# Cross-attention output and feed-forward in one block: first products by pieces, the last two chunk pairs as one down product, the final norm on VectorE

## The reference, cut to what matters

```python
x = x + cross_attend(...)                 # ends in o @ w_xo
h = rmsnorm(x, g_ffn)
a, g = h @ w_up, h @ w_gate               # 1024 -> 2816 each
c = conv_b + sum(ext[:, i:i+t] * conv_w[i] for i in range(3))   # ext = [prev, a]
x = x + (gelu(c) * g) @ w_down            # 2816 -> 1024
y = rmsnorm(x, g_final)
```

## Time and profile before

| | |
|---|---|
| median of 3 runs | 2283.32 us (2280.44 to 2283.92) |
| profiled execution, its own time | 2284.99 us |
| its span | 2283.0 us |
| mean granted clock of TensorE, as a share of 2.4 GHz | 0.952 |
| cross output, first to last product | 1341.8 to 1458.4 us |
| first matmul of the feed-forward | 1489.65 us |
| first down matmul behind the last gate product | 2201.96 us |

### The profile page before, as it was taken

How to read it: one execution, slowest core, us unless ns; L and a number is a source line. 1 busy time by engine, 2 the same in 40 slices (tenths; PEclk the granted TensorE clock), 3 DMA queues, 4 the chain that set the end, 5 groups by cost and what they waited for, 6 DMA issues and landing times. The chain is left out here.

```text
span 2283.0 us, 27161 instructions
## 1 busy us (share of the span) xinstructions
PE 2086.4 (91%) x10848; PEld 1661.7 (73%) x10848; DVE 794.5 (35%) x1804; ACT 544.1 (24%) x1226; POOL 253.3 (11%) x110
## 2 busy tenths in 40 slices
PE   7989989569999997998998899589999999999995
PEld 4555548357677775665667546389999999999994
DVE  3001132345555454351003212333433443433446
ACT  2112220035455555000002101121122111122113
POOL 0000000000000000000000001132233222233322
PEclk9999999779899898999999999799999999999997
DMA  5521017530010003012102420011111101111102
GB/s 198 138 84 42 0 59 185 146 125 24 23 46 23 23 0 129 1 38 110 46 28 111 184 94 0 0 60 38 56 56 56 47 29 38 56 56 56 47 14 76
DMA packets 96244, 144.96 MB, mean 63 GB/s; under 512 B 40877, under 2 KB 72685, under 8 KB 94253
## 3 DMA queue, kind: packets, MB, share of 16 engines
q1 hardware_dynamic: 92062, 140.43, 18.3%
q10 hardware_dynamic: 4088, 3.17, 0.5%
HBM read 132.43 MB, written 14.26 MB: 64 GB/s over the span
## 5 line engine op out<-in xcount | busy, mean ns | idle before, releaser
L1678 PE MATMUL ps<-ff_in_high,ff_weights_high 128*128 128x352 f32 x1056 | 341.8, 324 | 18.7 <-POOL ff_weights_low L1637 18.7
L1678 PE MATMUL ps<-ff_in_low,ff_weights_high 128*128 128x352 f32 x1056 | 339.5, 322 | 0.0
L1678 PE MATMUL ps<-ff_in_high,ff_weights_low 128*128 128x352 f32 x1056 | 339.2, 321 | 0.0
L1678 PEld LDWEIGHTS ps<-ff_in_high,ff_weights_high 128*128 128x128 f32 x1056 | 199.0, 188 | 19.7 <-POOL ff_weights_low L1637 19.7
L1678 PEld LDWEIGHTS ps<-ff_in_low,ff_weights_high 128*128 128x128 f32 x1056 | 199.2, 189 | 0.0
L1678 PEld LDWEIGHTS ps<-ff_in_high,ff_weights_low 128*128 128x128 f32 x1056 | 198.8, 188 | 0.0
L1806 DVE TENSOR_TENSOR x<-ps,x 128x352 f32<-128x352 f32 x264 | 138.2, 525 | 154.8 <-PE ps L1695 154.7
L935 PE MATMUL ps<-top,big 128*128 128x128 f32 (+1 forms) x1184 | 167.2, 289 | 13.2 <-ACT big L1037 7.2
L935 PEld LDWEIGHTS ps<-top,big 128*128 128x128 f32 (+1 forms) x1184 | 145.9, 194 | 32.3 <-ACT big L1037 15.5
L371 PE MATMUL ps<-big 128*128 128x512 f32 (+3 forms) x432 | 160.0, 532 | 6.2 <-DVE top L404 6.2
L1695 PE MATMUL ps<-ff_act_high,ff_down_high 128*128 128x352 f32 x480 | 154.9, 323 | 0.1
(11 more groups left out here) (276 smaller groups left out, 2887.1 us busy)
## 6 DMA issues: line engine op xcount, KB each, us to landing
ff_weights<-in_w_up SPq DMA_DIRECT2D x22, 512.0 KB, 4.1
ff_weights<-in_w_gate SPq DMA_DIRECT2D x22, 512.0 KB, 4.5
ff_down<-in_w_down SPq DMA_DIRECT2D x22, 512.0 KB, 3.6
x<-in_xt SPq DMA_DIRECT2D x6, 1408.0 KB, 12.1
big<-bias_rows SPq DMA_DIRECT2D x8, 960.0 KB, 4.6
top<-in_mem_kt SPq DMA_DIRECT2D x7, 1024.0 KB, 12.2
big<-in_w_tm SPq DMA_DIRECT2D x8, 652.0 KB, 16.2
top<-in_mem_v SPq DMA_DIRECT2D x5, 1024.0 KB, 17.2
```

Of the source, the lines that this page charges most:

```text
L1678: last = nc.tensor.matmul(K.bank[3 * s + x][:, 0:b - a], w[:, s, ws], h[:, k, a:b], start=k + n == 0, stop=k == KD - 1 and n == 2)
```

## The change

The two blocks become one function, `cross_output_and_ffn`. On each engine the code of the feed-forward follows that of the cross output with no meeting between.

- Join. The cross products go to banks 6, 7, 1, 4, the sum to bank 5. Chunk 0 is not made by `up_and_gate(0)`: for each piece x, as soon as `low_made` says it is split, PE makes the up and the gate part of that piece; the spread of piece 3 stands behind the products of piece 1. The weights of chunk 0 are split behind piece 1 of the norm (ACT and POOL). DVE signals `scaled` after each half of the 8 tiles, not after all. SP issues the first loads of the feed-forward after the last cross product.
- End. `down(9)` and `down(10)` become `last_down`: one product of 12 matmuls over four chunks for each output tile, over the four pieces `ENDS` (352, 352, 224 and 128 columns), in four banks. For the first four tiles nine of the twelve matmuls are made before the last chunk is ready.
- Final norm. Squares on ACT, all else on DVE (`norm.scale`, the 8 tiles with gain and root at once); ACT's gain multiply and POOL's part are gone. One transfer for each piece of y.

```diff
+ENDS = [(0, FREE3), (FREE3, 2 * FREE3), (2 * FREE3, 928), (928, T)]
...
+            sp.wait_ge(xo_done, PRODUCTS)
             sp.dma_start(prev, I["conv_prev"]).then_inc(small, 16)
...
-            for p, (a, b) in enumerate(PIECES[:2]):
-                sp.wait_ge(y, 2 * p + 2)
+            for p, (a, b) in enumerate(ENDS):
+                sp.wait_ge(norm.scaled, p + 1)
                 sp.dma_start(O["y"][:, :, a:b], K.XT[:, :, a:b]).then_inc(K.out_sem, 16)
...
+            def last_down():
+                chunks = tuple(range(FC - 4, FC))
+                pe.wait_ge(act_low, FC - 1)
+                pe.wait_ge(d_low_made, FC - 1)
+                pe.wait_ge(up_taken, FC)
+                for o in range(EARLY):
+                    if o == 3:
+                        pe.wait_ge(act_made, FC)
+                    down_part(K.bank[o], ENDS[0], o, chunks[:3], True, False)
+                pe.wait_ge(act_low, FC)
+                pe.wait_ge(d_low_made, FC)
+                for p in range(len(ENDS)):
+                    for o in range(KD):
+                        n = p * KD + o
+                        if n >= 4:
+                            pe.wait_ge(down_taken, LAST + n - 3)
+                        late = n < EARLY
+                        down_part(K.bank[n % 4], ENDS[p], o, chunks[3:] if late else chunks, not late, True).then_inc(down_done, 1)
+                        if p and o == 3:
                             norm.spread(pe, p - 1)
...
+            for x in range(3):
+                pe.wait_ge(low_made, 2 * x + 2)
+                for s, done in enumerate((up_done, gate_done)):
+                    last = products(0, s, x)
+                    if x == 2:
+                        last.then_inc(done, 1)
+                if x == 0:
+                    pe.wait_ge(added, PRODUCTS)
+                    xnorm.spread(pe, 2)
             up_and_gate(1)
-            for g in range(PAIRS - 1):
+            for g in range(PAIRS - 2):
                 up_and_gate(2 * g + 2)
...
+            up_and_gate(FC - 2)
+            up_and_gate(FC - 1)
+            last_down()
...
+            dve.wait_ge(down_taken, LAST)
+            for p, (a, b) in enumerate(ENDS):
+                for o in range(KD):
+                    n = p * KD + o
+                    dve.wait_ge(down_done, LAST + n + 1)
+                    nc.vector.tensor_tensor(K.XT[:, o, a:b], K.bank[n % 4][:, 0:b - a], K.XT[:, o, a:b], ALU.add).then_inc(down_taken, 1)
+                    if p and o == 1:
+                        norm.add_up(dve, p - 1)
+                    if p and o == 5:
+                        norm.scale(dve, p - 1, lambda c, a, b: K.XT[:, c, a:b])
```

More of the change, by code:

```diff
@@ L1262, in _ @@
                     last.then_inc(xq_done, 1)
[L1266 to L1330, removed]
@@ L1591, in ffn @@
     down_done, down_taken = S("ff_down_product"), S("ff_down_taken")
[L1592 to L1595, removed]
+    norm = FeatureNorm(nc, K, "fin", K.XT, K.gains[:, 5, :], ENDS, [sq], root, K.bank[5])
+    PRODUCTS = 3 * KD
     TILE = 3 * KD
-    LAST = (PAIRS - 1) * TILE
-    TAIL = 6
+    LAST = (PAIRS - 2) * TILE
+    EARLY = 4
     def down_place(c):
@@ L1659, in _, with products @@
                 activation(c)
[L1660 to L1665, removed]
         @block.tensor
         def _(pe):
+            def products(c, s, x):
+                a, b = PIECES[x]
+                for k in range(KD):
+                    ws = slice(k * P, (k + 1) * P)
+                    for n, (wt, h) in enumerate(((w_high, high), (w_high, low), (w_low, high))):
+                        last = nc.tensor.matmul(K.bank[3 * s + x][:, 0:b - a], wt[:, s, ws], h[:, k, a:b],
+                                                start=k + n == 0, stop=k == KD - 1 and n == 2)
+                return last
             def up_and_gate(c):
@@ L1671, in up_and_gate, with down_part @@
                     pe.wait_ge(low_done[s], c + 1)
[L1672 to L1679, removed]
-                    last.then_inc(done, 1)
+                    pe.wait_ge(taken, c)
+                    for x in range(3):
+                        last = products(c, s, x)
+                    last.then_inc(done, 1)
+            def down_part(bank, p, o, chunks, first, end):
+                a, b = p
+                at = slice(o * P, (o + 1) * P)
+                for e, c in enumerate(chunks):
+                    dh, dl = down_place(c)
+                    for m, (wt, x) in enumerate(((dh, a_high), (dl, a_high), (dh, a_low))):
+                        last = nc.tensor.matmul(bank[:, 0:b - a], wt[:, at], x[:, c % SLOTS, a:b],
+                                                start=first and e + m == 0, stop=end and c == chunks[-1] and m == 2)
+                return last
             def down(g):
@@ new lines, in _ @@
+            for p, (a, b) in enumerate(PIECES):
+                for c in range(KD):
+                    n = KD * p + c
+                    if p == 0:
+                        pe.wait_ge(w_came[c], 16)
+                    if n >= 4:
+                        pe.wait_ge(added, n - 3)
+                    for k in range(KD):
+                        last = nc.tensor.matmul(K.bank[(6, 7, 1, 4)[n % 4]][:, 0:b - a], w[:, c, k, :], K.HT[:, k, a:b],
+                                                start=k == 0, stop=k == KD - 1)
+                    last.then_inc(xo_done, 1)
+                    if p and c == 3:
+                        xnorm.spread(pe, p - 1)
```

215 lines of the change are left out of this document (107 added, 108 removed).

## The result

| | median of 4, us | lowest to highest | profiled run | its span | mean granted clock |
|---|---|---|---|---|---|
| before | 2281.88 | 2279.39 to 2283.92 | 2284.99 | 2283.0 | 0.952 |
| after | 2261.43 | 2258.05 to 2261.88 | 2261.88 | 2260.1 | 0.959 |

The ratio is 0.9908, 95% interval 0.9891 to 0.9925. I forecast 2253. 2261.43 lies inside the range of 2246 to 2268, outside the likeliest case's own 2247 to 2258. The gain between medians is 20.4 us where the sum said 30.4: 10.0 us are missing. Against the forecast of 2253 only 8.4 of them show, because the sum was taken off a median of 2283.32 and one more run of the kernel before brought that to 2281.88.

What follows compares the result with a forecast made beforehand. TensorE, busy 91% of 2283.0 us, bounds the kernel, so gains lie only where it waits or runs at half clock. Join 24.0 plus end 6.4 make 30.4 us off 2283.32, said as 2253; range 2246 to 2268, chance 0.84.

Steps and rivals of the forecast that it cites:

- the likeliest case: The prediction's own sum coming true: 2253 us, own range 2247 to 2258, chance 0.70.
- the sum: Join gain 24.0 us plus end gain 6.4 us, 30.4 us in all, taken off a median of 2283.32.
- Steps (1) to (6), the join: From the last cross product to the end of chunk 0: up pieces fill TensorE's idle time, gain 24.0 us.
- I cost that stretch at nothing: From 1515 to 2202 us TensorE is busy throughout; rows stay in their order, so no change to the 687 us.
- Is chunk 1 ready?: After the join, chunk 1's weights come in time, hidden by piece 3's gate part: no cost.
- The rival of a new wait at the join: Conv and GELU of chunk 0 or chunk 1's up weights come late: 2256 to 2261 us, chance 0.07.
- Step (9), the narrow price: At the end, fp32r matmuls of 224 or 128 columns cost 0.115 us each, all 192 of them 22.1 us.
- The rivals that priced it by an fp32 matmul's column or fixed cost: Narrow end matmuls: by column 0.38 and 0.23 us, time 2280, chance 0.12; fixed 0.597 us, time 2335, chance 0.04.
- Steps (10) and (11), the waits: In pieces 3 and 4 of the end, TensorE waits 1.1, 2.3, 1.9 and 0.8 us for adds, scalings and adding-up.
- The half clock of the narrow stretch: Close waits at the end halve the clock: narrow matmuls 0.235 us each, gain 15.6, time 2267.7, chance 0.07.
- steps (7) to (12): The end, from 2201.96 to the span's end: 2276.6 us against 2283.0, gain 6.4 us.
- Step (12), the tail: After the last products: scaling, adds, norm, reciprocal 0.94, eight scalings 2.2, to 2272.1, then transfer 4.5 us, end 2276.6.

## Why the forecast was right in its mechanism and 8 us off

- **Steps (1) to (6), the join: right.** From the end of the cross products to the end of chunk 0 I had 1491.05 - 1458.37 = 32.7 us; it took 34.3. The waits were 1.91 and 5.58 for 1.35 and 5.3: 0.9 us. Ahead of both, POOL's subtraction took longer, 6.72 and 6.64 where I took 6.25 from the earlier trace rows; it began while VectorE was still scaling, which there it did not, but no run tests that. Piece 3 took 10.55 us for 10.1, 0.4 more: 20 products at half clock for 18, the first of them 0.46 until the next. Pieces 1 and 2 and the spread add 0.2. The steps were right, the terms 1.6 us too small. (The kernel before ended chunk 0 at 1515.2 and not at 1515.0, so the gain is 1.4 short.)
- **"I cost that stretch at nothing": the step that failed in the middle.** The argument was that the rows stay in their order. They did, and cost 3.6 us more, because the block's new allocation moved their weights. The old kernel with one buffer moved shows such a loss; with this allocation taken back halfway, half of it returned. The 0.17 us between 45.79 and 45.96 stay unexplained, as does why an operand's place matters at all.
- **"Is chunk 1 ready?" at nothing: right.** The rival of a new wait at the join did not come.
- **Step (9), the narrow price: right,** 0.1115 for 0.115. The rivals that priced it by an fp32 matmul's column or fixed cost are out.
- **Steps (10) and (11), the waits: right while the clock stood.** Forecast 1.1, 2.3, 1.9 before the third tile of piece 3, the spread and the third tile of piece 4; TensorE's timeline has 0.87, 2.05 and 1.82 us idle. The last, of 0.8, was not there, because TensorE had become the late one.
- **The half clock of the narrow stretch, a rival at 0.07, came true in part: the step that failed in the end.** I argued against it with the wait of 1.70 us in the earlier trace rows that had left the clock up. The waits of 2.05 and of 1.82 were followed by it: 88 products at 0.213, not 192 at 0.235. Filled, the end is 6.4 us shorter (80.2 to 73.8), so the sum of steps (7) to (12) holds at full clock. A chance of 0.07 was far too low for a stretch whose waits I had just listed.
- **Step (12), the tail: its large terms were right** (reciprocal 0.95 for 0.94, eight scalings 2.19 for 2.2, adding-up 1.48 for 1.5), and the last transfer 4.0 for 4.5: from 2256.13, the end of the scalings, to 2260.1. The spread and root were 1.19 for 0.95.
- **The medians** agree with the profiles: 19.0 and 0.7 make 19.7 of the 20.4 us between them.
- **That 2261.43 lies inside the range** is in part the range's width. It was widened for rivals at 0.07 each, two misses of 5.0 and 5.7 us fit into it, and one of these, the placement, was in no rival.

What stays open: why these weights cost more at the far end of SBUF (other buffers move along in every such edit, so no run isolates the one address), and what exactly decides whether a wait of one to two us lowers the clock.

## What to carry to other kernels

A stretch that the diff leaves alone is not the same stretch if an allocation ahead of it changed: compare the addresses of the operands too, and read the time of a repeated block before and after. Where a change puts several short waits into TensorE's work, count the half clock as a case of its own, with matmuls from a row at half clock; unread matmuls in the waits keep it up, but too many become the new wait. Cutting a last piece smaller did not pay here even at full clock (73.8 us against 72.4): a matmul of 128 columns cost as much as one of 224, 0.1115 us.

## What the runs showed of the hardware that was not expected

- fp32r matmuls of 128 and of 224 columns cost the same, 0.1115 us at full clock and 0.213 at half; 352 columns 0.160 and 0.293.
- Once down among the 128-column products, the clock stayed at 0.50 from 2232.8 to 2249.2 with TensorE busy nearly throughout; at the join the 352-column products ran at half clock only from 1479.18 to 1484.75.
- The place of two weight buffers in SBUF (others move with them) changed 288 products from 45.79 to 46.67 us, 1.9%, with the instructions and their order unchanged.
- The same kernel's first cross product came between 1338.6 and 1341.3 us in two profiles, and between 1336.2 and 1342.3 over all: differences of 3 us between two profiles say nothing before the part that was not touched is taken off.
